# Second attention: transposes of heads and outputs moved in front of a unit's logits, exponential and row maximum

## The reference, cut to what matters

```
q, k, v = split(rmsnorm(h) @ w_in)          # 16 heads of 64
q, k = rmsnorm per head, times a gain
for each chunk c of 64 frames, keys = own chunk + 8 previous chunks:
    logits = q_c k_c^T * scale + bias(distance)   # outside the sequence: -inf
    p = softmax(logits);  o_c = p v_c
h = h + o @ w_out
```

## Time and profile before

| what | value |
|---|---|
| median of 3 runs | 2857.95 us |
| profiled execution, its own time | 2862.64 us |
| its span, first to last instruction | 2860.8 us |
| mean granted TensorE clock | 0.987 |
| PE busy | 2748.7 us (96%) |
| DVE busy | 1457.3 us (51%) |
| ACT busy | 1125.9 us (39%) |
| POOL busy | 829.6 us (29%) |

### The profile page before, as it was taken

One profiled execution on the slowest core, in us unless ns is written; L12 is line 12 of the kernel. 1 busy time (PEld: TensorE's weight loads), 2 busy tenths in 40 slices (PEclk: granted clock), 3 DMA queues, 4 the chain that ended last, 5 costly groups with the idle time before them and its releaser, 6 DMA issues. The chain is left out here.

```text
span 2860.8 us, 38670 instructions
## 1 busy us (share of the span) xinstructions
PE 2748.7 (96%) x14646; PEld 2380.9 (83%) x14678; DVE 1457.3 (51%) x2412; ACT 1125.9 (39%) x2409; POOL 829.6 (29%) x471
## 2 busy tenths in 40 slices
PE   7799999998999999999999998999989999999999
PEld 6598888987888888888889998888868888888887
DVE  5888766633544445444431126777235454444444
ACT  5676666632222222222245556666223222222221
POOL 2124433103323322333344441110133223322232
PEclk9899999999999999999999999999999999999999
DMA  5110000101111111111031100002011111111111
GB/s 171 45 45 7 21 9 8 64 30 59 45 45 44 58 45 44 44 59 44 37 115 45 45 23 7 27 12 80 30 52 46 50 44 44 56 46 51 44 51 59
DMA packets 38754, 132.43 MB, mean 46 GB/s; under 512 B 4240, under 2 KB 12608, under 8 KB 36960
## 3 DMA queue, kind: packets, MB, share of 16 engines
q1 hardware_dynamic: 38624, 130.68, 13.8%
HBM read 122.22 MB, written 13.69 MB: 48 GB/s over the span
## 5 line engine op out<-in xcount | busy, mean ns | idle before, releaser
L367 PE MATMUL banks<-XH,WH 128*128 128x512 f32 x1408 | 441.5, 395 | 18.8 <-POOL WL L314 12.6
L367 PE MATMUL banks<-XL,WH 128*128 128x512 f32 x1408 | 441.8, 395 | 0.0
L314 POOL TENSOR_TENSOR WL<-WR,WH 128x1024 fp32r<-128x1024 f32 x132 | 330.0, 2507 | 379.4 <-ACT WH L260 379.4
L367 PE MATMUL banks<-XH,WL 128*128 128x512 f32 x1408 | 438.7, 393 | 0.0
L275 ACT ACTIVATE Y<-U,CONVB,CONVW 128x1024 f32<-128x1024 f32 x88 | 109.5, 1245 | 639.8 <-DVE U L415 639.8
L367 PEld LDWEIGHTS banks<-XH,WH 128*128 128x128 f32 x1408 | 266.2, 190 | 78.0 <-POOL WL L314 13.4
L415 DVE TENSOR_TENSOR U<-banks,RB 128x1024 f32<-128x1024 f32 x88 | 107.7, 1224 | 417.2 <-PE banks L367 403.6
L367 PEld LDWEIGHTS banks<-XH,WL 128*128 128x128 f32 x1408 | 266.4, 189 | 61.1
L367 PEld LDWEIGHTS banks<-XL,WH 128*128 128x128 f32 x1408 | 266.5, 189 | 58.2
L405 DVE TENSOR_TENSOR XT<-XT,banks 128x1024 f32<-128x1024 f32 x176 | 214.4, 1218 | 164.6 <-PE banks L383 164.6
L322 POOL TENSOR_TENSOR AL<-Y,AH 128x1024 fp32r<-128x1024 f32 x44 | 106.3, 2417 | 611.7 <-ACT AH L283 611.7
(11 more groups left out here) (251 smaller groups left out, 5519.6 us busy)
## 6 DMA issues: line engine op xcount, KB each, us to landing
WR<-in_ffn SPq DMA_DIRECT2D x132, 512.0 KB, 3.5
QWR<-in_qkv SPq DMA_DIRECT2D x8, 1536.0 KB, 6.7
XT<-in_xT SPq DMA_DIRECT2D x16, 512.0 KB, 7.5
OWR<-in_w_o SPq DMA_DIRECT2D x16, 512.0 KB, 3.3
QWR1F<-in_qkv SPq DMA_DIRECT2D x4, 1536.0 KB, 6.4
spill<-XT SPq DMA_DIRECT2D x8, 512.0 KB, 10.9
XT<-spill SPq DMA_DIRECT2D x8, 512.0 KB, 7.8
outT<-XT SPq DMA_DIRECT2D x8, 512.0 KB, 2.6
```

Source lines behind the costliest of these rows:

```text
L314: pool.tensor_tensor(WL[:, ch % RING, :], WR[:, ch % RING, :], WH[:, ch % RING, :].bitcast(F32), ALU.subtract).then_inc(w_lo, 1)
L367: mm = pe.matmul(u[:, h * HALF:(h + 1) * HALF], w[:, ch % RING, db * P:(db + 1) * P], x[:, db, h * HALF:(h + 1) * HALF], start=(db == 0 an ...
```

## The change

On each of the three engines the lines for the round through `TQ` are put in front of the line for unit g+3 (PE, DVE) or g+2 (ACT). Nothing is added or left out.

```diff
@@ band_phase, ACT
-                if g + 2 < ALL:
-                    exp(g + 2)
                 if tile_of(g) is not None:
                     heads_high(tile_of(g), rounds_before(g))
                 if output_of(g) is not None:
                     output_high(output_of(g), rounds_before(g))
+                if g + 2 < ALL:
+                    exp(g + 2)
@@ band_phase, PE
-                if g + AHEAD < ALL:
-                    logits(g + AHEAD)
                 if tile_of(g) is not None:
                     heads(tile_of(g), rounds_before(g))
                 if output_of(g) is not None:
                     output(output_of(g), rounds_before(g))
+                if g + AHEAD < ALL:
+                    logits(g + AHEAD)
@@ band_phase, DVE
-                if g + AHEAD < ALL:
-                    row_max(g + AHEAD)
                 if tile_of(g) is not None:
                     heads_low(tile_of(g), rounds_before(g))
                 if output_of(g) is not None:
                     output_low(output_of(g), rounds_before(g))
+                if g + AHEAD < ALL:
+                    row_max(g + AHEAD)
```

## The result

The changed kernel takes 2864.81 us (median of 20 runs, 2860.87 to 2868.95), the kernel before 2860.21 us on the same chips (20 runs, 2856.7 to 2865.86). The medians differ by 4.6 us. The ratio is 1.0014 with a 95% interval of 1.0008 to 1.0021: about +4.0 us, 2.3 to 6.0. The forecast was +3.5 us, no difference by the 0.3% bound, on the slow side of it.

The account below looks back on a forecast made before the run. Pairs of tiles 3 to 7 were taken as bound by a ring of waits across PE, ACT and DVE. Its terms summed to +0.50 us a group, 7 x 0.50 = +3.5 on 2857.95, giving 2861.5 us; range 2849 to 2871.

Parts of the forecast that it names:

- The ring: Second attention's unit loop: heads, `QS`, `KH`, low queries, `KL`, copy, turn, values, logits, heads set the pair's pace, 5.45 us.
- A logits leaves, a row maximum enters: Pairs of tiles 3 to 7: logits of 0.71 us leave the ring, row maximum of 0.75 enters; +0.50 us a group.
- The term of tile 6: Pair of tile 6: row maximum of 640 columns enters, logits of 128 leave, 0.75 - 0.26 = +0.49 us.
- those of tiles 3 to 5: Pairs of tiles 3, 4, 5: 0.75 - 0.71 = +0.04 us each, +0.12 together.
- ACT's move costs nothing: `exp` behind `KH` on ACT costs nothing; the exponential of unit g+2 has over 0.8 us to spare before its reader.
- Unpriced loads of the transposes: Heads' transposes behind 64-column values on PE: exposed weight loads could cost or save 3.6 us; taken as 0.
- PE's own way: PE's own work would reach the turn at +3.58 us after the heads, earlier than the ring's +3.88, so the ring binds.
- Tiles 0 to 2 unchanged: Pairs of tiles 0 to 2: heads to output stays the 2.55 us chain, so the change adds 0.
- Rival A: Copy of `PT` in time, logits leave, nothing enters: the 11.9 us of turn waits go, 2846.0 us; chance 0.13.
- Rival B: Late `turned_lo` holds the heads, so the row maximum enters and logits don't leave: 22.5 us, 2880.4 us; chance 0.09.
- Rival C: PE's clock falls at the longer tile 0 stall for 6 us in each of 7 groups: 12 us, 2873.4; chance 0.06.
- Rival D: Nothing moves, tile 6 pair included, because the ring has overlooked slack: 2858 us; chance 0.10.

Follow-up runs that it names:

- the late row maximum: Changed kernel with the row maximum of every even unit that has heads put behind the odd unit's copy of `PT` on DVE: 2849.38 us, ratio 0.9961.
- the first two experiments: Kernel before with the new order on PE only: 2892.0 us; kernel before with the new order on DVE only: 2909.51 us.

## Why the prediction was right, point by point

- **The ring** as the bound of pairs of tiles 3 to 7: shown. Each of its stations came within 0.02 us of the forecast, and taking the row maximum out of it (tile 6, then all) moved just the pairs that the ring says, to within 0.11 us of the expected lengths.
- **A logits leaves, a row maximum enters**: shown from both sides. DVE alone puts the row maximum in without taking the logits out, and large pairs grow by 0.75; the late row maximum takes it out, and they fall to PE's own work. Taking a logits out was never shown by itself, since PE alone ran into other waits. But the changed kernel lies under DVE alone by 0.71 us at tiles 4 and 5, by 0.24 at tile 6 and by 0.31 at tile 7, and the logits that leave there were priced at 0.71, 0.26 and 0.32. The term of tile 6, +0.49, measured +0.50 and is nearly the whole sum; those of tiles 3 to 5, +0.04 each, measured +0.03 to +0.04; tile 7, -0.11, measured -0.10.
- **ACT's move costs nothing**: right for the change, and shown alone but for the two pairs of group 4. That it is needed with DVE's was only touched in the walk; it is worth some 22 us.
- **Unpriced loads of the transposes**, taken as 0 between -3.6 and +3.6: ten values are followed by the heads after 1.06 us (1830.63 to 1831.69), where logits followed after 1.03, so 0.03 a pair, 1 us in all. By the figure of the Trainium skill (TensorE: Matmul & The Clock Gate, LDWEIGHTS) for a load of 128 columns the estimate of the sum was +7.2 us; the trace shows no whole load exposed.
- **PE's own way**, put at +3.58 for the turn, is +3.45 (measured with the row maximum out of the ring): the heads hold the queue 0.09 us less than assumed. The ring still binds, with a margin of 0.42 instead of 0.30.
- **The total.** That +4.0 us lies so near +3.5 is partly luck, since the interval is 2.3 to 6.0. What bears the forecast out is the lengths of the pairs. The profiled loop grew by only 2.2 us, and nothing shows where the rest of the 4.0 lies.
- **Tiles 0 to 2 unchanged**: right, within 0.04.
- **Rival A** (faster) did not happen in the change, since DVE's queue is in order, but its 11.9 us was the right price: the late row maximum won 11. The range's lower end, 2849, is not half way into this rival as the prediction says; half way between 2861.5 and 2846.0 is 2853.7.
- **Rival B** (the row maximum enters, the logits stay) did not happen; DVE alone showed its price a pair exactly.
- **Rival C** (the clock) did not happen in the profiled execution of the changed kernel: its stall at tile 0 grew from 1.27 to 1.44 us (0.10 more was forecast) and the clock stayed at 2.4 GHz. It did happen in four experiments, in one of them behind the very same work of PE (next section). So that it stayed away here is in part luck, and whether it did in the other 19 executions is not shown.
- **Rival D** (nothing moves) is ruled out by the pair of tile 6, 5.00 to 5.50 us, and by the interval, which lies above 1.

What failed was my walk for PE alone and, in part, for DVE alone. In both I followed the ring that binds in the change and not the other waits that the half-made change brings near: the output's wait for `KL`, the heads' wait for `XL`, and ACT's queue behind an exponential. The 28 and 49 us were not in any expectation.

## What the runs showed of the hardware

The granted clock fell in the unit loop without any long pause of PE. Windows view, first the kernel before, then the changed kernel, each 8 us over tiles 0 and 1:

```profile
1804.00:1812.00 8.00, 5.90 (x46) 4.88 (x44) 4.91 (x17) 5.27 (x19) 1.23 (x2) 1.00 0.00 0
```

```profile
1803.00:1811.00 8.00, 5.54 (x44) 4.95 (x43) 4.83 (x16) 5.19 (x18) 1.23 (x2) 1.00 0.00 0
```

With PE alone changed, the same tiles and what followed:

```profile
1816.00:1824.00 8.00, 4.71 (x36) 4.12 (x36) 4.37 (x14) 4.90 (x15) 1.23 (x2) 1.00 0.00 0
1824.00:1828.00 4.00, 3.52 (x20) 3.12 (x17) 2.05 (x8) 2.44 (x6) 0.61 (x1) 0.64 0.00 0
```

No stall in these 8 us was longer than 1.44 us, but PE was busy for 4.71 of them only, and then the clock was at the 1.2 GHz level for part of the next four: pair 2 took 6.15 us. With DVE alone changed it stayed there for 16 us, although PE was busy for 15.33 of them:

```profile
1763.00:1779.00 16.00, 15.33 (x71) 14.69 (x71) 5.78 (x22) 6.75 (x23) 1.79 (x3) 0.50 0.05 19
```

PE's busy share does not tell the falls from the rest. In the kernel with the late row maximum of tile 6 alone, PE runs the same instructions up to tile 0 as in the changed kernel, with the same longest stall of 1.44 us. Its clock fell there in one group of the profiled execution, that of the changed kernel did not. First the changed kernel, the 8 us into its stall and the 4 us behind them, then the other:

```profile
1798.00:1806.00 8.00, 6.22 (x54) 5.78 (x53) 4.37 (x16) 4.26 (x15) 1.23 (x2) 1.00 0.14 48
1806.00:1810.00 4.00, 2.97 (x21) 2.65 (x22) 2.75 (x10) 2.74 (x9) 0.62 (x1) 1.00 0.00 0
```

```profile
1801.00:1809.00 8.00, 6.22 (x54) 5.77 (x54) 4.73 (x18) 4.88 (x17) 1.23 (x2) 1.00 0.17 50
1809.00:1813.00 4.00, 4.00 (x19) 3.69 (x19) 1.93 (x8) 2.53 (x9) 0.61 (x1) 0.57 0.00 0
```

PE was busy for 6.22 of 8 us in both; then one kept 1.00 and the other had 0.57. This group took 38.5 us instead of 37.6. What decides between the two, these runs do not show. They show only how often it came: behind the loop's first microseconds, in one group here, in none with the changed kernel, in three with DVE alone, in four with PE and DVE and in six with PE alone, one profiled execution each.

The Trainium skill (TensorE: Matmul & The Clock Gate, Part 1) states that the gate goes back to half rate after PE was idle. No run here has a long pause in the loop to test that on. What the traces add is that the clock can fall behind stalls of 1.44 us and less, and need not. So a wait in a loop that is already loose can cost more than its own length, and the sums of the first two experiments, which left the clock out, came out too low for that reason too.

## What to carry to other kernels

When lines are exchanged in hand-ordered queues of several engines, write down the ring of waits that sets the pace and ask, for each engine, what leaves the ring and what enters it: here 0.71 us left on PE and 0.75 entered on DVE, and the width of the next tiles decided the rest. An instruction that used to run in a wait for nothing costs its whole length once it stands behind the wait; put it behind the last instruction that somebody else waits for (here the copy of `PT`), and the early start is kept. Such moves can't be tried one by one: of the change's parts, PE's alone lost 28 us, DVE's alone 49, both without ACT's 26, and ACT's alone did nothing, where all three together lost 4.
